# Two layers of a hybrid diffusion backbone: half-size fillers in the attention, an interleaved start of the output projection, bias rows read from PSUM, and another unit order in the second layer's head

## What is computed

```python
for l in range(2):
    last = l == 1
    mx = split(silu(c) @ mod_w[l] + mod_b[l], 9)       # shift, scale, gate per sub-layer; mh from c_ctx
    x = x + 0.5 * mx[2] * swiglu(modulate(rms_norm(x, norm_ffn1[l]), mx[0], mx[1]), ...)
    h = h + 0.5 * mh[2] * swiglu(...)
    ux, uh = modulate(rms_norm(x or h, norm_mix[l]), ...)
    # one input projection: Fourier f (256), GQA q (512), k, v (128 each),
    # neighbourhood nq, nk, nv (256 each), three gates (1024 each)
    y_f = fourier_mix(f) @ w_fourier
    y_g = gqa(rope(rms(q)), rope(rms(k)) + context keys) @ w_gqa_out
    y_n = neighbourhood_attention(nq, nk, nv, context, rpb) @ w_na_out
    yx = (g_f * y_f + g_g * y_g + g_n * y_n) @ w_o     # g = sigmoid(gate logits)
    x = x + mx[5] * yx
    x = x + 0.5 * mx[8] * swiglu(...)                  # second FFN
    if not last: h goes through the same steps
return rms_norm(x, final_norm)
```

## Time and profile before

| | us |
|---|---|
| median of 3 runs | 2025.54 (2023.0 to 2025.99) |
| profiled execution, its own time | 2022.01 |
| its span | 2020.2 |
| PE busy | 1962.2 (97%) |
| POOL busy | 1006.0 (50%) |
| DVE busy | 773.1 (38%) |
| ACT busy | 655.2 (32%) |

### The profile page before, as it was taken

One profiled execution on the slowest core, in us unless ns is written; L12 is line 12 of the kernel. 1 busy time (PEld: TensorE's weight loads), 2 busy tenths in 40 slices (PEclk: granted clock), 3 DMA queues, 4 the chain that ended last, 5 costly groups with the idle time before them and its releaser, 6 DMA issues.

```text
span 2020.2 us, 29286 instructions
## 1 busy us (share of the span) xinstructions
PE 1962.2 (97%) x10550; PEld 1609.4 (80%) x10550; DVE 773.1 (38%) x1278; ACT 655.2 (32%) x1031; POOL 1006.0 (50%) x835
## 2 busy tenths in 40 slices
PE   6999999999999999999999999999999899999998
PEld 4777777787667888877877887788778677998998
DVE  4322122357762224623122353221233875564214
ACT  3211211243452223412211243222123444444433
POOL 2444444343213544545544445454445433988997
PEclk9999999999999999999999999999999999999999
DMA  9555655343112333553354236434523422655664
GB/s 338 171 179 181 195 189 181 122 113 108 43 43 64 102 94 94 172 183 114 117 165 129 72 112 224 159 96 142 179 67 105 142 75 58 183 166 158 184 181 131
DMA packets 413575, 279.25 MB, mean 138 GB/s; under 512 B 25346, under 2 KB 398588, under 8 KB 406060
## 3 DMA queue, kind: packets, MB, share of 16 engines
q1 hardware_dynamic: 401868, 206.79, 34.6%
q10 hardware_dynamic: 11520, 71.05, 9.6%
q0 software_dynamic: 96, 0.16, 0.0%
HBM read 276.92 MB, written 1.05 MB: 138 GB/s over the span
## 4 chain that ended last, share of the span: by engine, by line
PE 84%; POOL 5%; issue 5%; DVE 4%; DMA 1%; ACT 1%; SPq 0%; POOLq 0%; DVEq 0%; ACTq 0%
PE bank L1286 26%; PE bank L1287 26%; PE bank L1288 25%; POOL w_lo L494 5%; PE bank L1395 3%; DVE u_lo L943 1%; PE bank L1653 1%; PE bank L1635 1%; PE bank L1588 1%; DMA w_raw<-in_ffn_w_in 1%; DVE tmp L930 1%; DVE rstd L1112 1%; PE bank L1535 1%; DVE qk L1103 0%; SPq L403 0%
## 5 line engine op out<-in xcount | busy, mean ns | idle before, releaser
L494 POOL TENSOR_TENSOR w_lo<-w_raw,w_hi 128x512 fp32r<-128x512 f32 (+2 forms) x824 | 1003.4, 1247 | 1003.0 <-ACT w_hi L526 1002.2
L1286 PE MATMUL bank<-u_hi,w_hi 128*128 128x512 f32 (+2 forms) x2008 | 723.2, 360 | 16.6 <-DVE u_lo L943 12.4
L1287 PE MATMUL bank<-u_lo,w_hi 128*128 128x512 f32 (+2 forms) x2008 | 713.7, 355 | 0.0
L1288 PE MATMUL bank<-u_hi,w_lo 128*128 128x512 f32 (+2 forms) x2008 | 712.9, 355 | 0.0
L1286 PEld LDWEIGHTS bank<-u_hi,w_hi 128*128 128x128 f32 x2008 | 380.6, 190 | 97.1 <-DVE hf L999 21.0
L526 ACT ACTIVATE w_hi<-w_raw 128x1024 fp32r<-128x1024 f32 (+2 forms) x412 | 385.3, 968 | 178.1 <-PE bank L1288 164.3
L1288 PEld LDWEIGHTS bank<-u_hi,w_lo 128*128 128x128 f32 x2008 | 380.5, 189 | 53.9
L1287 PEld LDWEIGHTS bank<-u_lo,w_hi 128*128 128x128 f32 x2008 | 380.9, 190 | 52.3 <-issue 0.8
L999 DVE TENSOR_TENSOR hf<-bank,sg 128x512 f32<-128x512 f32 (+1 forms) x85 | 53.2, 625 | 613.5 <-ACT sg L628 613.5
L1286 PE MATMUL bank<-h_hi,w_hi 128*128 128x512 f32 (+1 forms) x704 | 256.0, 364 | 0.0
L1287 PE MATMUL bank<-h_lo,w_hi 128*128 128x512 f32 (+1 forms) x704 | 255.4, 363 | 0.0
(11 more groups left out here) (170 smaller groups left out, 1523.7 us busy)
## 6 DMA issues: line engine op xcount, KB each, us to landing
w_raw<-in_ffn_w_in SPq DMA_DIRECT2D x176, 512.0 KB, 3.8
mod_w<-in_mod_w ACTq DMA_DIRECT2D x56, 1024.0 KB, 6.9
w_raw<-in_w_in SPq DMA_DIRECT2D x68, 512.0 KB, 3.7
w_raw<-in_ffn_w_out SPq DMA_DIRECT2D x64, 384.0 KB, 3.4
w_raw<-in_ffn_w_out SPq DMA_DIRECT2D x64, 320.0 KB, 3.3
mod_first<-in_mod_w SPq DMA_DIRECT2D x4, 2048.0 KB, 14.3
mod_w<-in_mod_w ACTq DMA_DIRECT2D x16, 512.0 KB, 5.5
w_raw<-in_w_o SPq DMA_DIRECT2D x16, 512.0 KB, 4.2
```

Of the source, the lines that this page charges most:

```text
L494: pool.tensor_tensor(w_lo[:, slot, k0:k1, :], w_raw[:, slot, k0:k1, :], w_hi[:, slot, k0:k1, :].bitcast(F32), ALU.subtract).then_inc(S("w_ ...
L1286: pe.matmul(dst, w_hi[:, slot, kk, :], hi_, start=start, stop=False)
L1287: pe.matmul(dst, w_hi[:, slot, kk, :], lo_, start=False, stop=False)
L1288: return pe.matmul(dst, w_lo[:, slot, kk, :], hi_, start=False, stop=stop)
```

## The change

There are four edits, and bookkeeping that follows from them. (1) A filler may be cut in two halves of 12 matmuls, and a third place for fillers, `middle`, comes between the scores and the second transposes. (2) In the second layer v and nk0 stand as the second pair of the head, f0 and f1 behind them, then q1 to q3; the order of the small steps on PE, ACT and DVE changes with it. (3) The bias rows of the first norm are read from PSUM (bank 4) instead of `vec`. (4) The first two units of the output projection are interleaved by input tile, the second of them in bank 6, and ACT converts the following weights one unit earlier.

```diff
+    HEADS = [FEW + F + MANY + V + NK + NQ + NV, FEW + V + NK[:1] + F + MANY + NK[1:] + NQ + NV]
+    QKS = [[0, 1, 4, 5, 6], [0, 1, 6, 7, 8]]
...
         if l == DEPTH - 1:
-            return [([nk0], [nk1]), ([nq0], [nq1]), ([nv0], [("vt", 1)]), ([nv1], [("vt", 2)]), ([g0], []), ([g1], []), ([g2], [])]
-        return [([nk0], [nk1]), ([], []), ([nq0], []), ([], []), ([nq1], []), ([], []),
-                ([nv0], [("vt", 1)]), ([nv1], [("vt", 2)]), ([g0], []), ([], []), ([g1], []), ([], []), ([g2], [])]
+            return [([], [nk1], []), ([], [nq0], [nq1]), ([], [nv0], []), ([], [vt1], [nv1a]),
+                    ([], [nv1b], [vt2, g0a]), ([], [g0b], [g1a]), ([g1b], [g2a], [g2b])]
+        return [([], [nk0], [nk1]), ([], [nq0a], []), ([], [nq0b], []), ([], [nq1a], []), ([], [nq1b], []),
+                ([], [nv0a], []), ([], [nv0b], [vt1]), ([], [nv1a], []), ([], [nv1b], [vt2]),
+                ([], [g0a], []), ([], [g0b], []), ([], [g1a], []), ([g1b], [g2a], [g2b])]
...
+            rows = vec if k else vec_bank
+            gain = rows[:, l, V_N1 + DC * w + d0:V_N1 + DC * w + d1]
+            dve.tensor_tensor(colB[:, k, :, d0:d1], modcol[:, l, :, b0:b1], both(rows[:, l, b0:b1]), ALU.add)
...
@@ ACT, head of the second layer
+                square_head(0)
+                square_head(1)
+                hi_ahead(6)
+                copy_head(2, vT[:, 0, :], 2).then_inc(S("head_copied"), 1)
+                copy_head(3, nqk[:, 0, :], 3).then_inc(S("head_copied"), 1)
+                hi_ahead(7)
+                root_head(0)
+                copy_head(4, fT[:, 0, :], 0).then_inc(S("head_copied"), 1)
+                hi_ahead(8)
+                root_head(1)
...
@@ DVE, head of the second layer
+                raw(0)
+                raw(1)
+                head_norm(0)
+                head_norm(1)
+                rope(0)
+                spectrum(0)
+                raw(2)
+                rope(1)
+                raw(3)
+                spectrum(1)
+                head_norm(2)
+                raw(4)
+                fourier(0)
+                head_norm(3)
+                rope(2)
+                fourier(1)
+                rope(3)
...
@@ PE, head of the second layer
+                statistics(0)
+                unit(4, 0)
+                statistics(1)
+                unit(5, 1)
+                swap(0)
+                channels(0)
+                unit(6, 2)
+                swap(1)
+                channels(1)
+                unit(7, 3)
+                statistics(2)
+                unit(8, 0)
+                positions(0)
+                statistics(3)
+                swap(2)
+                positions(1)
+                swap(3)
...
@@ ACT, output projection
+            ahead = [(ph, q) for q in range(2, DC)] + [(nph, q) for q in range(3)]
+            hi(ph, 0, 1)
             for m in range(DC):
-                if m + 2 < DC:
-                    hi(ph, m % 2, (m + 2) // 2)
-                elif m + 2 == DC:
-                    first_hi(following(key))
+                p_, q = ahead[m + 1]
+                hi(p_, q % 2, q // 2)
...
@@ PE, output projection
+            for kk in range(DC):
+                if kk in (0, LO_SPLIT):
+                    pe.wait_ge(S("w_lo_ready"), goals[1] * 2 + (2 if kk else 1))
+                pe.wait_ge(S("mg_ready"), MG0 + kk + 1)
+                for j in range(2):
+                    last = three(bank[:, wo_bank(j), 0:n], slots[j], kk, mg_hi, mg_lo, kk, n, kk == 0, kk == DC - 1)
+                    if kk == DC - 1:
+                        last.then_inc(S("w_used"), 1)
+            for m in range(2, DC):
+                pe.wait_ge(S("x_done"), m0 + m - 1)
+                products(ph, m % 2, m // 2, 0, 2, bank[:, wo_bank(m), 0:n], mg_hi, mg_lo, 0, n, True, True)
```

More of the change, by code:

```diff
@@ L510, in _ @@
             elif key[1] == "head":
-                for idx in range(len(HEAD)):
+                for idx in range(len(HEADS[l])):
                     lo(ph, idx, 0)
@@ L1206, in _ @@
             NP = len(js) // 2
-            for p, (before, after) in enumerate(between(l)):
+            for p in range(len(between(l))):
                 for up in (0, 1):
@@ L1269, in _, with products @@
     def _(pe):
-        def products(ph, j, c, i, per, dst, hi_, lo_, k0, n, start, stop, k_wait=None):
+        def products(ph, j, c, i, per, dst, hi_, lo_, k0, n, start, stop, k_wait=None, part=None):
             slot, g, _ = ph.at(j, c, i, per)
             nk = ph.kd[j]
-            for kk in range(nk):
+            for kk in range(*(part or (0, nk))):
                 if kk in (0, LO_SPLIT):
@@ L1590, in scores @@
                             last.then_inc(S("s_ready"), 1)
-            bank7 = [u for before, after in between(l) for u in before + after]
+            bank7 = [u[0:2] for parts in between(l) for part in parts for u in part if u[2] == 0]
             def bank7_free(u):
-                at = bank7.index(u)
+                at = bank7.index(u[0:2])
                 if at == 0:
@@ L1654, in values @@
                 last.then_inc(S("o_ready"), 1)
-            for p, (before, after) in enumerate(between(l)):
+            for p, (middle, before, after) in enumerate(between(l)):
                 if p == 1:
@@ L1662, in _ @@
                     scores(p)
+                for u in middle:
+                    fill(u)
                 if p == 0:
```

265 lines of the change are left out of this document (148 added, 117 removed).

## The result

| | before | after |
|---|---|---|
| median, us | 2023.4 (2020.1 to 2026.5, 20 runs) | 2027.8 (2025.7 to 2030.3, 20 runs) |
| ratio of after to before, 95% interval | | 1.0023 (1.0017 to 1.0029) |
| profiled execution, its own time and span | 2022.0, 2020.2 | 2025.7, 2023.9 |
| granted clock, mean of the execution | 0.996 | 0.993 |

The change makes the kernel slower by 0.23%, 4.4 us, which is just over what a measurement of it can tell. To see where, I cut both spans at rows that every variant has: the start row of a PE instruction in each of them, and the difference of its position between the two traces.

A forecast was written before the change was run, and what follows sets the result against it. PE, busy 97% of the span, bounds the kernel, so edits only remove or add its waits. Terms -1.05 + 2.5 - 1.0 + 2.4 - 1.4 + 0.35 = +1.8 us on 2025.5 gave 2027.3; whole range 2020 to 2033.

The forecast's parts named there:

- start: Bias rows in PSUM: DVE 1.9 us earlier, PE's gain limited by a modulation-weight load; -1.05 us, bounds 0 and 2.3 gained.
- steps 2 and 3; 4 and 5: First layer's attention: half fillers make odd steps wait 1.3 for `copy_pt`, the 1.0 before the values goes; +0.3 us each pair.
- steps 8 and 9: First layer's attention: DVE can't be earlier, so all 2.7 us become waiting and 1.0 is saved; +1.7 us.
- steps 10 and 11: First layer's attention: as in steps 8 and 9, 2.7 us of new waiting for DVE less 1.0 saved; +1.7 us.
- seven more cuts: First layer's attention: switching in and out of cut fillers, about 0.1 us per cut; +0.7 us.
- second layer's head: Waits for `u_lo` shrink, new waits come from ACT's order and DVE; -1.0 us, between -4.3 and +2.
- second layer's attention: End waits go, but vt1, nv1, vt2, g0 and g1 wait for ACT's copies; +2.4 us, between -5 and +4.
- merge, second and first layer: Output projection: interleaving covers the last `mg_lo`, earlier conversion removes POOL's idle time; -1.4 us second layer, +0.35 first.
- Both signs that I had named for being wrong: No bracket on odd steps' second transposes, or a granted clock of 0.50 at places other than the profiled one.
- The covers could do the work: Rival: copies are ready when PE arrives, first layer -6.5 instead of +2.5; 2018.3 or about 2020 us; chance 0.22.
- the second rival: The clock falls behind new waits of 2.4 to 2.9 us at six places; three falls give +6.3, 2031.8; chance 0.26.
- Whether the start gives its gain or none: Rival: the start gives nothing since PE waits for the load; 2028.3 us, within the forecast's range, no chance given.

The follow-up runs named there:

- experiment 5: The changed kernel, with DVE in the first layer doing `to_cat` and the mask's addition behind the awaited copy: 2024.0 against the kernel before's 2022.7, ratio 1.0003.
- experiment 3: The changed kernel with the second layer's head back in the old order, the new attention order kept: 2027.7 against the kernel before's 2023.1, ratio 1.0024.
- experiments 1 to 4: One comparison undoing parts of the change: first-layer fillers 2026.3, second-layer fillers 2024.8, second-layer head 2027.7, all three 2021.8, against the kernel before's 2023.1.
- 5 and 6: The changed kernel with `to_cat` and mask addition behind the copy, 2024.0; that plus unevenly cut first-layer fillers, 2018.8; the kernel before 2022.7.
- experiment 10: The kernel before with the bias rows' edit alone: 2021.4 against 2023.6, ratio 0.9991 (0.9982 to 1.0000).
- experiment 9: The changed kernel with DVE reordered, uneven first-layer cuts, second-layer head mended, nq0 and `rope(4)` moved earlier: 2008.3 against the kernel before's 2023.6, ratio 0.9923.
- experiment 12: The kernel of experiment 9 with the old merge, two units one after the other and ACT's old order: 2009.6, ratio 0.9928 to the kernel before.

## Why the prediction was right or wrong

The forecast was 2027.3 and 0.50 for a change within 0.2%; the median is 2027.8. That closeness is partly luck, and the measured 0.23% lies just outside the 0.2% to which the 0.50 was given. My step was +1.8 us on a base of 2025.5, the median of three runs. Over twenty runs the kernel before has 2023.4, and the change costs 4.4. On the profiled executions, which is what the sum was made for, it is +3.7 against +1.8. The terms, measured with their cuts inside:

| term | predicted | profile |
|---|---|---|
| start | -1.05 | -1.4 |
| step 1 | -1.0 | -1.0 |
| steps 2 and 3; 4 and 5 | +0.3 each | +0.2; +0.3 |
| steps 6 and 7 | +1.0 | +1.2 |
| steps 8 and 9 | +1.7 | +2.95 |
| steps 10 and 11 | +1.7 | +1.75 |
| last step | -2.2 | -1.9 |
| seven more cuts | +0.7 | (inside) |
| first layer's attention, sum of the rows from step 1 on | +2.5 | +3.4 |
| second layer's head | -1.0 | +0.9 |
| second layer's attention | +2.4 | +1.7 |
| merge, second and first layer | -1.4, +0.35 | -1.1, +0.35 |

(A pair's length is from the first transposes of one even step to those of the next, less 5.66 us for a whole filler in it and 2.83 for a half. The head ends at the transposes behind nq1.) The start's -1.4 is a single draw: over all profiled executions the stretch is 0.3 us shorter with the edit than in the one without it.

**What held.** The argument on covers in steps 2 to 5: a half taken from an even step comes back as waiting for `copy_pt`, 2.22 and 1.34 us, with the sizes given, and experiment 5 shows the cause, `to_cat` and the mask's addition ahead of the copy. Some places held too: 0.87 for nv0's copy, 2.93 before `swap(3)`, 1.29 for `update(0)`.

**What came elsewhere.** In steps 8 and 9 I had all of the 2.7 us as waiting for DVE before the second transposes. They have no wait; PE waits 2.34 us in step 8 for nv1's copy, which I had seen for nv0 and not for nv1. The size was about right, and the wait was another. In steps 10 and 11 the 2.7 is split, 1.27 for normalise and 1.47 for `copy_pt`. In the second layer's head the waits of 1.1 before `statistics(1)` and 1.6 before `swap(0)` did not come (PE worked at half clock from 1600.2 on), and `rope(4)` is waited for 1.50 and not 2.4: by the brackets the waits there went from 5.3 to 7.4 us, where I had 7.3 and 11. Both signs that I had named for being wrong were therefore seen, no bracket in step 9 and a granted clock of 0.50 at 576, 1627 and 1801 us. The total came out near because fewer waits and more half clock met.

**Terms that were mis-sized.** The cut: two halves take 2.94 + 2.93 against 5.66 for a whole, 0.21 and not 0.1 for each. In the merge the interleaving was to cover the last `mg_lo`; it waits 1.42, since I priced POOL's presence on `mg_lo` (two SBUF inputs) and not on `mg_hi`, 0.29 us without POOL and 1.16 under it.

**The step that failed** is the weight of the clock. I named six waits of 2.4 to 2.9 us, gave the falls behind them a case of their own, and left them out of the likeliest sum. Three new waits of 2.2 us and more came, and two of them had a fall in this profile: in step 8 (+1.25 over the term; transposes, scores and v tile take 1.6 us more than before) and at `swap(3)` (eight scores took 3.79 us instead of 1.99, and the head's 1.9 over the term is of that size). That such falls belong into the sum can be counted: in the fourteen profiled executions a fall began within, or less than 2 us behind, 13 of the 15 waits of 2.7 us and more, and 14 of the 29 waits of 2.0 to 2.35. But a fall's price hangs on what follows it, as experiment 3 shows: there the fall at `swap(3)` was gone and nothing came back, so the head's excess can't be given to the clock alone. The runs show it without profiles as well: the mean granted clock is 0.9932 over the changed kernel's twenty executions and 0.9946 over 33 of the kernel before, 27 against 22 us at half clock (twice the missing share of 2022 us), 5.4 more. (The 33 are those of experiments 1 to 4's comparison.) At half speed PE loses at most half of such time, so that the clock has at most 2.7 of the 4.4 us; a fall in dense work cost 1.5 us (the last part of the span has 227.4 to 227.5 us in five executions with one at the start of the feed-forward part, and 225.9 to 226.0 in four without). The runs of one kernel among themselves say the same: over the 90 runs of the kernel before in the experiments the span grows by 1.35 us with each 0.001 of mean clock that is missing, which makes 1.8 us for the 0.0013 here. And at the same mean clock the change is still slower: its spans average 2025.6 us against 2023.6 at 0.993, and 2025.0 against 2022.1 at 0.994. What is left, 2 to 3 us, is about my sum. This split is an estimate, not shown: no run holds the waits and moves only the clock.

I also read one execution too literally. The profile of before, with two falls, was a good one (its mean clock 0.9956, its runs' 0.9946), and the same code fell at 531 us in three kernels and not in the change's own profile. The Trainium skill ("TensorE: Matmul & The Clock Gate", section "What's actually happening") says it of a kernel's start: the number of matmuls at the low clock is run-variable, since it depends on the phase of the activity monitor when the kernel starts. In these executions it holds for waits in the middle too (a wait of 2.22 at 529 us with the clock at 1.00 behind it, the same wait with 0.50 in three others).

**The rivals.** The covers could do the work, as that rival said, but not in this change: they did once DVE's order was mended (5 and 6). The clock did fall, as the second rival said, but with fewer new waits than I had counted, and the change came out between that rival's +6.3 and my sum. Whether the start gives its gain or none experiment 10 can't tell.

## What to carry to other kernels

Filling PE's waits with smaller pieces gained nothing here while the engine that PE waits for had its own order wrong: look first at what stands ahead of the awaited instruction on that engine, move what nobody waits for behind it, and only then size the pieces to each step's wait. A long wait costs more than its length where the clock falls with it, and the falls move from run to run; so compare the sum of waits and the mean clock over many runs, not the places of falls in two profiles. In experiment 9, where one wait of 2.0 us is the longest between the second norm and the last 8 us, the time fell by 15 us, and five runs lie within 1.6 us, against 6.1 for the 21 of the kernel before; with a wait of 2.2 more (experiment 12) five lie within 2.7.

## What was unexpected of the hardware

- A cast with one SBUF input was slowed fourfold by POOL: `mg_hi`, 128x256, 293 ns in seven of eight and 1159 in the one that ran under a conversion; 294 ns in the same place with POOL idle. The Trainium skill says it ("SBUF — State Buffer", section "Who interferes with whom": a cast may enter a mode that takes the pair of ports shared with GpSimd), and I had read only the line on two inputs.
- A wait of 1.1 and one of 0.9 us shortly behind it were followed by half clock at 532 us in one execution and not in four others, and a single 2.22 at 529 us was in three and not in one. Of the 46 falls in the middle of the profiled executions 19 came with no wait of 2.0 us or more.
- A filler of 24 matmuls cut in two costs PE 0.2 us more with 512 columns (2.94 + 2.93 against 5.66) and next to nothing with 256 (two halves take 1.53 and 1.54, a whole one 3.04).
